# Scores of two heads issued back to back from opposite row halves, in the indexed and the differential attention

## What is computed

```python
def dsa_attention(q, k, v, q_idx, k_idx, w_idx):      # 8 heads of 64
    ...
    s = jnp.einsum('bqhd,bqkhd->bhqk', qb, ks).astype(jnp.float32) * (d ** -0.5)
    s = jnp.where(valid[:, :, None, :], s, -jnp.inf)
    p = jax.nn.softmax(s, axis=-1).astype(vs.dtype)
    return jnp.einsum('bhqk,bqkhd->bqhd', p, vs)
...
def odd_mixer(...):
    qs = jnp.concatenate([q[..., :C_QK_DIM], q[..., C_QK_DIM:]], axis=2)   # 4 heads x 2 halves of 64
    ks = jnp.concatenate([k[..., :C_QK_DIM], k[..., C_QK_DIM:]], axis=2)
    o = causal_attention(qs, ks, jnp.concatenate([v, v], axis=2), C_QK_DIM ** -0.5)
    ...
    c = rms_norm(o[:, :, :C_HEADS] - lam * o[:, :, C_HEADS:], subln) * (1.0 - lam_init)
```

## Time and profile before

| | |
|---|---|
| time, median of 3 runs | 2732.92 us (2729.94 to 2734.82) |
| span of the profiled execution | 2725.5 us, 28695 instructions |
| TensorE busy | 2672.6 us, 98% |
| VectorE busy | 1259.9 us, 46% |
| ScalarE busy | 658.4 us, 24% |
| mean granted TensorE clock | 0.995 |
| stage "a" / stage "c" (by where L1165 runs) | 130.3 to about 310 us / 500 to about 592 us |

### The profile page before, as it was taken

One profiled execution on the slowest core, in us unless ns is written; L12 is line 12 of the kernel. 1 busy time (PEld: TensorE's weight loads), 2 busy tenths in 40 slices (PEclk: granted clock), 3 DMA queues, 4 the chain that ended last, 5 costly groups with the idle time before them and its releaser, 6 DMA issues.

```text
span 2725.5 us, 28695 instructions
## 1 busy us (share of the span) xinstructions
PE 2672.6 (98%) x11362; PEld 1773.7 (65%) x11362; DVE 1259.9 (46%) x2490; ACT 658.4 (24%) x1491; POOL 60.1 (2%) x116
## 2 busy tenths in 40 slices
PE   8999999999999999999999999999999999999999
PEld 4445557656478888746556664655555684788886
DVE  5733333444334456425363426465564451344564
ACT  2122331246200000222342123525252202000001
POOL 0000000000000000000000001011010000000000
PEclk9999999999999999999999999999999999999999
DMA  4211012100122222120110131121120411222222
GB/s 156 76 48 62 31 64 82 61 32 10 66 80 93 93 93 70 69 93 32 62 62 32 64 124 55 39 78 47 62 76 34 177 62 62 92 93 93 81 74 78
DMA packets 120445, 194.88 MB, mean 71 GB/s; under 512 B 5148, under 2 KB 61272, under 8 KB 119416
## 3 DMA queue, kind: packets, MB, share of 16 engines
q1 hardware_dynamic: 118848, 180.82, 19.6%
q0 software_dynamic: 1344, 12.19, 1.2%
q10 hardware_dynamic: 120, 0.03, 0.0%
HBM read 185.69 MB, written 7.34 MB: 71 GB/s over the span
## 4 chain that ended last, share of the span: by engine, by line
PE 96%; ACT 2%; DVE 1%; issue 1%; DMA 0%; ACTq 0%; DVEq 0%
PE psum L532 20%; PE psum L529 15%; PE psum L2312 14%; PE psum L418 9%; PE psum L2294 8%; PE psum L403 6%; PE psum L438 5%; PE psum L1165 2%; PE psum L2162 2%; PE psum L455 2%; PE psum L1185 2%; PE psum L462 1%; PE psum L1173 1%; PE psum L660 1%; PE psum L391 1%
## 5 line engine op out<-in xcount | busy, mean ns | idle before, releaser
L2312 PE MATMUL psum<-weight_ring,h_t 128*128 128x512 f32 x896 | 409.0, 600 | 3.1 <-ACT arena L2593 1.9
L585 DVE TENSOR_TENSOR arena<-arena,psum 128x512 f32<-128x512 f32 x179 | 122.9, 687 | 346.7 <-PE psum L532 287.6
L2312 PEld LDWEIGHTS psum<-weight_ring,h_t 128*128 128x128 f32 x896 | 163.3, 192 | 165.8 <-issue 162.4
L418 PE MATMUL psum<-h_t,weight_ring 128*128 128x512 f32 x544 | 235.6, 594 | 2.2 <-DVEq L3032 0.8
L2294 PE MATMUL psum<-h_t,weight_ring 128*128 128x512 f32 x512 | 233.0, 598 | 0.9 <-DVE arena L2912 0.9
L532 PE MATMUL psum<-h_t,weight_ring 128*128 128x256 f32 x1024 | 228.2, 380 | 0.0
L529 PE MATMUL psum<-weight_ring,arena 128*128 128x256 f32 x992 | 222.2, 382 | 2.3 <-ACT arena L2722 1.5
L532 PEld LDWEIGHTS psum<-h_t,weight_ring 128*128 128x128 f32 x1024 | 194.9, 190 | 27.1 <-issue 1.3
L529 PEld LDWEIGHTS psum<-weight_ring,arena 128*128 128x128 f32 x992 | 189.9, 192 | 28.8 <-issue 3.3
L418 PEld LDWEIGHTS psum<-h_t,weight_ring 128*128 128x128 f32 x544 | 102.9, 190 | 130.9 <-issue 128.9
L403 PE MATMUL psum<-weight_ring,h_t 128*128 128x512 f32 (+1 forms) x384 | 162.3, 580 | 0.8 <-DVEq L1640 0.8
(11 more groups left out here) (409 smaller groups left out, 3407.6 us busy)
## 6 DMA issues: line engine op xcount, KB each, us to landing
weight_ring<-in_ffn_w_in_dram SPq DMA_DIRECT2D x44, 1024.0 KB, 6.8
weight_ring<-in_w_in_dram SPq DMA_DIRECT2D x20, 2048.0 KB, 7.8
weight_ring<-in_ffn_w_out_dram SPq DMA_DIRECT2D x8, 2048.0 KB, 7.9
weight_ring<-in_w_in_even_dram SPq DMA_DIRECT2D x7, 2048.0 KB, 8.2
weight_ring<-in_w_in_odd_dram SPq DMA_DIRECT2D x5, 2048.0 KB, 7.8
weight_ring<-in_w_in_dram SPq DMA_DIRECT2D x8, 1024.0 KB, 7.0
weight_ring<-in_w_branch_gdn_dram SPq DMA_DIRECT2D x4, 2048.0 KB, 7.8
weight_ring<-in_ffn_w_out_dram SPq DMA_DIRECT2D x4, 1536.0 KB, 6.9
```

What stands on the lines that cost most here:

```text
L418: last = pe.matmul(bank, slot[:, k, c:c + P], act[:, k, :], start=(k == 0), stop=(k == KD - 1))
L585: ins = dve.tensor_tensor(out, other, bank, op)
L2312: last = pe.matmul(bank, act[:, k, t * P:(t + 1) * P], slot[:, k, :], start=(k == 0), stop=(k == KD - 1))
```

## The change

`pe_attention` gets an argument `together`. With 2, as in "a" and "c", the scores of steps m and m+1 are issued one behind the other at every even m, after the waits for both banks, and none at odd m. The lists of steps are put in another order: a pair of heads (in "c" the two halves of a head) for one query block, then the next block; so nk goes 128, 128, 256, 256, 384, 384, 512, 512, and the two scores of a pair stand in opposite row halves. VectorE's and ScalarE's loops aren't edited and follow the new list. "m" keeps `together=1`.

```diff
-def pe_attention(K, pe, tag, steps, bufs, beside=None):
+def pe_attention(K, pe, tag, steps, bufs, beside=None, together=1):
+
     _, probs, probs_t = bufs
     n_steps, base = len(steps), K.att_base[tag]
     for m in range(n_steps + 2):
-        if m < n_steps:
-            q, k = steps[m]["q"], steps[m]["k"]
-            bank = K.next_bank((tag, "s", m))
-            if K.turn((tag, "s", m)) > 1:
-                pe.wait_ge(K.free_of((tag, "s", m)), K.turn((tag, "s", m)) - 1)
-            pe.matmul(bank[:, 0:k.shape[-1]], q, k, start=True, stop=True).then_inc(K.full_of((tag, "s", m)), 1)
+        if m < n_steps and m % together == 0:
+            scored = range(m, m + together)
+            banks = [pe_fresh(K, pe, (tag, "s", n)) for n in scored]
+            for n, bank in zip(scored, banks):
+                q, k = steps[n]["q"], steps[n]["k"]
+                pe.matmul(bank[:, 0:k.shape[-1]], q, k, start=True, stop=True).then_inc(K.full_of((tag, "s", n)), 1)
         if 1 <= m <= n_steps:
             i = m - 1
             pe.wait_ge(K.probs_ready, base + i + 1)
...
 def even_steps(K, V):
     steps = []
-    for h in range(A_H):
-        p, ct = 64 * (h % 2), h // 2
-        for i in range(NT):
-            nk = (i + 1) * P
+    for ct in range(A_H // 2):
+        for i, par in ((i, par) for i in range(NT) for par in range(2)):
+            h, p, nk = 2 * ct + par, 64 * par, (i + 1) * P
...
-    pe_attention(K, pe, "a", even_steps(K, V), V["att"], beside)
+    pe_attention(K, pe, "a", even_steps(K, V), V["att"], beside, 2)
...
 def diff_steps(K, V):
     steps = []
     for h in range(C_H):
-        for half, out in ((0, "o1"), (1, "o2")):
-            p = 64 * half
-            for i in range(NT):
-                nk = (i + 1) * P
+        for i in range(NT):
+            for half, out in ((0, "o1"), (1, "o2")):
+                p, nk = 64 * half, (i + 1) * P
...
-    pe_attention(K, pe, "c", diff_steps(K, V), V["att"], beside_diff)
+    pe_attention(K, pe, "c", diff_steps(K, V), V["att"], beside_diff, 2)
```

## The result

| | time before, median | time of this kernel, median | ratio to the kernel before, 95% interval |
|---|---|---|---|
| the changed kernel | 2730.96 us (13 runs) | 2740.07 us (13 runs, 2735.12 to 2742.5) | 1.0026, 1.0019 to 1.0033 |
| the same kernel, measured again | 2732.31 us (19 runs) | 2739.67 us (9 runs) | 1.0025, 1.0014 to 1.0035 |

The account below looks back on a forecast made before the run. TensorE's own instructions in a row were taken as the bound. "a": -14.2 + 14.4 = +0.2; "c": -14.2 + 15.4 + 0.5 + 0.6 = +2.3; together +2.5 us, so 2735.4 us, range 2729 to 2743.

Parts of the forecast that it names:

- Pairs cost one score: TensorE's scores in "a" and "c": both halves run together, so 16 scores go per stage, 14.2 us saved in each.
- The bank turn: At even iterations o(m-2) needs the bank of o(m-3), freed behind a mask: 14 waits per stage, "c" 15.4 us, "a" 14.4.
- The price of a wait from scores to o: Per wait, scores to out's end less TensorE's time to o, plus the return: 0.72 to 1.23 us in "c".
- 0.16 more: Return after each wait for the out: 0.06 us until the weight load, 0.10 for a load not pulled ahead.
- 3.56 us for each group: TensorE's saving per eight steps without second scores, from 0.57, 0.79, 1.00 and 1.20 by nk; 28.5 us in all.
- 0.5 for rotations: Iterations 4 to 11 of "c": VectorE rotates between two masks, delaying o at odd m; 0.5 us, bounds nothing and 2.8.
- 0.6 for the exponential: First two pairs of "c": transposes come before the exponential ends; 0.3 to 0.4 and 0.2 to 0.3 us.
- The signs that the forecast named: Profile marks: TensorE busy some 20 us less, span within 5, o idle 0.3 to 0.9, "a" unchanged, "c" 1 to 4 longer.
- Rival 1: Out comes later and more waits appear in "c"; rotations 2.8, each return 0.1 more: +7.6, 2740.5 us; chance 12%.
- Rival 2: New idle times in "a" and "c" make TensorE's clock fall, seven falls costing 12 us: +14.5, 2747 us; chance 8%.
- Rival 3: VectorE writes the out early, waits are shorter; with half of each gone -12.4, 2720.5 us; chance 7%.
- Rival 4: Paired scores run one after the other, mostly absorbed by the waits: +3.8, 2736.7 us; chance 3%.

## Why the prediction was off by its size and right in its mechanism

**Pairs cost one score: right.** The x4 rows take 0.42 to 1.06 us to the transposes, as the x2 rows of before did. Where both scores of a pair come from one row half, those of 512 columns take 1.91 instead of 1.06. That is a factor of 1.8 and not quite the full 2, since the 0.2 us of the two changes of shape is paid either way.

**The bank turn brings 14 waits in each stage, in even iterations, ended by VectorE's out: right.** Shown from two sides: another bank takes them away with VectorE's order untouched, and another order on VectorE takes them away with the banks untouched.

**The price of a wait from scores to o: right to 0.02 us; what comes behind it was missing.** The forecast let a return cost 0.06 + 0.10. It costs 0.12 until the load, because two semaphores are waited for, 0.03 from the load to o (555.93 to 555.96), and the o behind takes 0.07 more: from 550.22 to the fill at 551.18 it is 0.96 us, where the eight instructions took 0.89 before (from 534.96 to the fill at 535.85). So the term "0.16 more" of the step on the added wait should have been about 0.22. The run with one semaphore gives the 0.06 back, and there the forecast's 0.16 is met. Over 28 waits it is 1.7 us, of which 1.6 is shown by that run.

**"3.56 us for each group" was too much in "a".** The forecast took the costs of scores in "c" for both stages. In "a", late iterations have work of the retention with 64 rows beside them, and the change from 128 rows to 64 is paid there in any case. TensorE's timeline of one such place, first before, then changed:

```profile
261.25 0.72 PE L1460 MATMUL psum<-arena 64*128 64x128 f32 x8
261.79 0.59 PE L1165 MATMUL psum<-arena 64*128 64x256 f32 x2
262.32 0.33 PE L1173 MATMUL psum<-consts_sb,arena 128*128 128x128 f32 x1
```

```profile
263.57 0.72 PE L1460 MATMUL psum<-arena 64*128 64x128 f32 x8
264.22 0.33 PE L1174 MATMUL psum<-consts_sb,arena 128*128 128x128 f32 x1
```

From L1460 to the transposes it took 1.07 us with a score between and takes 0.65 without: 0.42 saved, where the forecast has 0.79. Over the six odd iterations from 21 to 31 such differences, read in the same way, add up to 1.3 us. The run with the out first shows the same amount from the other side: "a" without waits saves 12.9, not 14.2.

**The sum, redone.** "a": the forecast +0.2, and 1.3 of saving that isn't there, and 14 x 0.06 = 0.9 of returns: +2.4, measured +2.3. "c": the forecast +2.3 and 0.9 of returns: +3.2, measured +3.2. Together +5.6 against +5.5, where the forecast had +2.5. In "c" the smaller saving that the run with own banks showed (3.13 per group) doesn't appear in the changed kernel: there the fill is followed by its transposes after 0.86 again, presumably since the wait ahead of it has given the exponential its time. The forecast's 0.5 for rotations and 0.6 for the exponential show one by one in the first steps of the changed kernel:

```profile
505.38 1.12 PE L2311 MATMUL psum<-weight_ring,h_t 128*128 128x512 f32 x2
506.63 0.33 PE L1174 MATMUL psum<-consts_sb,arena 128*128 128x128 f32 x1
...
515.79 0.49 PE L1174 MATMUL psum<-consts_sb,arena 128*128 128x128 f32 x3
516.34 0.68 PE L1186 MATMUL psum<-arena 128*128 128x128 f32 x4
```

The transposes that wait for the exponential start 1.25 us behind the fill instead of 0.86, and in the second pair 1.02 (508.77 to 509.79): 0.39 and 0.16 late, 0.55 in sum. Iteration 5, with rotations between the two masks, has its o 0.55 behind the transposes, where 0.33 is usual (563.05 to 563.38). With smaller pieces of the same kind in iterations 5, 6, 7 and 11 that makes about 0.55. The second of these agreements is partly luck: the forecast took 0.5 out of bounds of 0 and 2.8.

**From the stages to the total.** +5.5 of a measured 7.1 (interval 5.2 to 9.0). The 1.6 between them is within the interval, so no further cause of the change's own is needed, and none is excluded either. One candidate is the clock outside the stages: its mean is 0.9929 over the 22 timed runs of the changed kernel and 0.9933 over the 47 runs of the kernel before for which it is listed. By an estimate that lets TensorE be the bound throughout, this is about 1 us. Whether the change has a part in that isn't shown.

**The signs that the forecast named.** TensorE's busy time fell by 17.5 us (some 20 were named) and "c" grew by 3.2 (1 to 4). Three were missed: the span grew by 8.1 us (at most 5), "a" by 2.3 (it was to stay as long), and the idle entries of o are 0.5 to 1.1 us (0.3 to 0.9). The time of 2740.07 us also lies at the edge of the forecast's own spread (2731 to 2740); it is the allowance for the rivals that put it well inside the range.

**Rival 1** (2740.5 us) came nearest by its number, and half by its mechanism: each of the returns cost more, 0.06 and not 0.1, but no more waits appeared in "c", and the rotations cost what the likeliest case had for them.

**Rival 2, the clock, falls.** Both stages ran at 1.00 through 28 idle times of 0.5 to 1.1 us. There are slow stretches elsewhere, and they lie in other places from one execution to the next. In the changed kernel one is right behind "a" (TensorE's clock is the column after the engines, 0.79):

```profile
314.00:330.00 16.00, 13.37 (x38) 6.43 (x37) 9.50 (x33) 6.94 (x9) 0.00 (x0) 0.79 0.39 133
```

The same stretch of the kernel in which only the order of steps is new, without any of the waits:

```profile
314.00:330.00 16.00, 14.26 (x29) 6.36 (x30) 7.63 (x22) 5.37 (x5) 0.00 (x0) 0.79 0.38 133
```

It is there too, and that kernel isn't slower than before. The kernel before has the same idle time of 1.65 us at this place (its transposes start at 314.00), and its clock stayed at 1.00 until 381. The Trainium skill (TensorE: Matmul & The Clock Gate, A second HAM failure mode: psum-queue depth-cycling) reports a bf16 kernel whose clock kept falling and rising in this way, and by it rival 2 would have been the forecast. In these runs repeated short idle times between groups did not bring the clock down in either stage.

**Rival 3, the gain comes, didn't, for the reason given**: VectorE can't pass the mask in its own queue. Let it write the out first, and the gain is there (2709.4 us). **Rival 4, serial pairs, is false for this kernel**, and its statement that the wait would absorb the second score is confirmed: 24 serial pairs cost 0.8 us in both stages together, where 9.4 show without the waits.

**The remark on PSUM.** The Trainium skill (TensorEngine Tiling (Array Packing), PSUM Bottleneck) names the emptying of PSUM as what tiling doesn't speed up, and as a possible bottleneck after a speedup of four; the pairs here give at most two. With the same instructions in another order VectorE gets the two stages done 28.1 us sooner than in the changed kernel (22.6 sooner than before). The rate wasn't the limit; which bank is emptied first was.

## What to carry to other kernels

When instructions that take banks or buffers in turn are grouped, write down for each taker who had its place before and where the freeing instruction stands in its own engine's queue; here that list gave all 28 waits before the run. A consumer that has been idle for microseconds may still free a bank too late, if it takes the new work first and the old work second: try the other order, or another bank for the one tile in question, before giving up the grouping. And price a saving in each place where it is to occur: beside neighbours of the same shape it is smaller, and behind a wait it is absorbed, so that even serial pairs cost nothing that the total could show.

## What the runs showed of the hardware that was not expected

- A matmul released after a wait on two semaphores started its weight load 0.12 us after the releasing instruction ended, with one semaphore 0.06 (555.81 to 555.93; 556.65 to 556.71). Dropping the redundant wait 28 times gave 1.6 us.
- The length of a stage repeats to 0.03 us between executions in which its clock is undisturbed, while totals spread by 7 us. Most of the spread is made by the slow stretches of the clock, which move: in the timed runs of the changed kernel the time is 2734.8 to 2735.7 us at a mean granted clock of 0.995 and 2739.7 to 2742.7 at 0.992. A tenth of a per cent can be read in a stage where the total can't show it.
- The idle entries of o were 0.54 to 1.04 us in the group shown, some 0.2 less than the wait that was worked out (0.72 to 1.23), since the ends in TensorE's rows are modelled and overhang.
